# Halves of frequencies in the inverse long convolution, norms tile by tile, one merged sum on VectorE

## The reference

```
h     = rmsnorm(x) * (1 + scale1) + shift1
cq, ckv, kr, hy_in, gates = split(h @ w_in)          # 384, 256, 32, 1536, 2048 columns
q     = rmsnorm(cq) @ w_uq;  kv = rmsnorm(ckv) @ w_ukv;  kr and q's last 32 columns rotated
attn  = softmax(q k^T) v                              # 8 heads, latent: 512 queries, 640 keys
y     = v-part of short_conv(hy_in)
for o in (0, 1):                                      # bidirectional, by FFT of twice the length
    y = gate_part[o] * long_conv(y, filter[o])
merged = sigmoid(g_a) * (attn @ w_oa) + sigmoid(g_b) * (y @ w_ob)
x     = x + gate1 * (merged @ w_out)
h2    = rmsnorm(x) * (1 + scale2) + shift2
x     = x + gate2 * peer(h2)                          # 8 heads x top-16 of 128*128 single-neuron experts
```

## Time and profile before

| | us |
|---|---|
| three runs, median (lowest to highest) | 4708.16 (4695.34 to 4711.38) |
| the profiled execution, its own time | 4711.11 |
| its span | 4709.3 |
| PE busy | 3782.0 (80%) |
| DVE busy | 3191.0 (68%) |
| POOL busy | 2091.9 (44%) |
| ACT busy | 1563.4 (33%) |
| mean granted clock of TensorE, of full speed | 0.924 |

### The profile page before, as it was taken

How to read it: one execution, slowest core, us unless ns; L and a number is a source line. 1 busy time by engine, 2 the same in 40 slices (tenths; PEclk the granted TensorE clock), 3 DMA queues, 4 the chain that set the end, 5 groups by cost and what they waited for, 6 DMA issues and landing times.

```text
span 4709.3 us, 42094 instructions
## 1 busy us (share of the span) xinstructions
PE 3782.0 (80%) x12598; PEld 2025.1 (43%) x12598; DVE 3191.0 (68%) x7297; ACT 1563.4 (33%) x4531; POOL 2091.9 (44%) x1771
## 2 busy tenths in 40 slices
PE   7988799897797777767877789989698777777776
PEld 4547574446453333324533356446554232232222
DVE  1322778786898876666567768977788875755555
ACT  2321341001343444443333333100244444444444
POOL 2240355573344444454344455556144444444443
PEclk8889899998899888988989899999799899999999
DMA  7556478795899989999999877867699999999998
GB/s 276 201 205 220 174 242 304 282 354 215 327 420 406 392 364 401 417 409 380 376 421 422 317 254 262 334 240 290 233 410 412 395 416 420 418 414 421 422 421 344
DMA packets 268416, 1604.74 MB, mean 341 GB/s; under 512 B 31686, under 2 KB 34034, under 8 KB 112540
## 3 DMA queue, kind: packets, MB, share of 16 engines
q0 software_dynamic: 234880, 1395.89, 74.8%
q1 hardware_dynamic: 33308, 206.16, 11.3%
HBM read 1590.62 MB, written 11.30 MB: 340 GB/s over the span
## 4 chain that ended last, share of the span: by engine, by line
PE 34%; DMA 30%; DVE 22%; issue 5%; ACT 5%; POOL 4%; SPq 0%; DVEq 0%; ACTq 0%; POOLq 0%
DMA sb_arena<-in_peer_uv,sb_idx 14%; PE ps L1157 12%; DMA sb_gbufs<-in_peer_uv,sb_idx 11%; DVE sb_gbufs L1977 4%; PE ps L1053 4%; DVE sb_arena L1977 3%; PE ps L1094 3%; PE ps L1071 3%; DVE sb_eacc L2002 2%; POOL sb_gbufs L2223 2%; PE ps L761 2%; DMA sb_gbufs<-in_peer_uv,sb_idx_v 2%; DMA sb_ring<-in_w_oab 2%; PE ps L734 1%; ACT sb_small L1443 1%
## 5 line engine op out<-in xcount | busy, mean ns | idle before, releaser
L1157 PE MATMUL ps<-sb_gbufs,sb_dge 128*128 128x512 f32 x1836 | 909.0, 644 | 293.1 <-ACT sb_dge L1464 288.5
L1157 PE MATMUL ps<-sb_arena,sb_dge 128*128 128x512 f32 x1832 | 884.1, 631 | 248.9 <-ACT sb_dge L1464 248.8
L2237 POOL DMA_INDIRECT sb_gbufs<-in_peer_uv,sb_idx x512 | 624.9, 1221 | 890.0 <-PE ps L1157 737.4
L2237 POOL DMA_INDIRECT sb_arena<-in_peer_uv,sb_idx x512 | 615.1, 1201 | 747.5 <-PE ps L1157 648.4
L1977 DVE CUSTOM_DVE_ANT_0 sb_gbufs<-sb_gbufs,sb_keep 128x1024 f32<-128x1024 f32 x512 | 625.6, 1234 | 368.7 <-DMA sb_gbufs<-in_peer_uv,sb_idx 366.7
L1977 DVE CUSTOM_DVE_ANT_0 sb_arena<-sb_arena,sb_keep 128x1024 f32<-128x1024 f32 x512 | 622.4, 1229 | 340.6 <-DMA sb_arena<-in_peer_uv,sb_idx 338.9
L1157 PEld LDWEIGHTS ps<-sb_gbufs,sb_dge 128*128 128x128 f32 x1836 | 360.0, 205 | 804.3 <-ACT sb_dge L1464 407.1
L1157 PEld LDWEIGHTS ps<-sb_arena,sb_dge 128*128 128x128 f32 x1832 | 352.7, 200 | 746.3 <-issue 374.8
L1440 ACT ACTIVATE sb_small<-sb_small 128x2 f32<-128x2 f32 x512 | 104.1, 203 | 1503.2 <-DVE sb_small L1977 1499.6
L2223 POOL DMA_INDIRECT sb_gbufs<-in_peer_uv,sb_idx x256 | 322.2, 1259 | 324.0 <-DVE sb_small L1977 139.0
L2223 POOL DMA_INDIRECT sb_gbufs<-in_peer_uv,sb_idx_v x256 | 334.7, 1307 | 238.4 <-DVE sb_eacc L2002 181.2
(11 more groups left out here) (278 smaller groups left out, 4285.6 us busy)
## 6 DMA issues: line engine op xcount, KB each, us to landing
sb_ring<-in_w_wq SPq DMA_DIRECT2D x48, 1024.0 KB, 7.1
sb_keep<-in_w_ada POOLq DMA_DIRECT2D x52, 512.0 KB, 6.1
sb_ring<-in_w_hy SPq DMA_DIRECT2D x24, 1024.0 KB, 8.2
sb_ring<-in_w_oab SPq DMA_DIRECT2D x18, 1024.0 KB, 8.5
sb_ring<-in_w_ga SPq DMA_DIRECT2D x16, 1024.0 KB, 7.1
sb_ring<-in_w_gb SPq DMA_DIRECT2D x16, 1024.0 KB, 8.7
sb_ring<-in_w_out SPq DMA_DIRECT2D x14, 1024.0 KB, 8.2
sb_gbufs<-in_peer_uv,sb_idx POOLq DMA_INDIRECT x768, 10.2
```

The costliest lines, as they stand in the source:

```text
L1157: q = pe.matmul(ps[:, c, :], dge[:, b, :], gbuf[b][:, D + c * 512:D + c * 512 + 512], start=(h == 0 and i == 0), stop=(h == HALVES - 1 and ...
L2237: nc.gpsimd.indirect_dma_start(out=gbuf[b], out_offset=None, in_=I["peer_uv"], in_offset=bass.IndirectOffsetOnAxis(ap=idx[:, n + SLOTS:n + ...
```

## The change

Three edits.

1. In both layers' latent group, each inverse long convolution goes by halves of frequencies: for all 4 blocks of channels the matmuls of kc = 0, once that half's spectrum is there (`Yc` o*2+1); then for all 4 those of kc = 1 (`Yc` o*2+2), with the event `y_ps` after each block. The 32 matmuls, their operands and weights are the same; the four banks are all claimed ahead of the second half.
2. The query and key norms of the latent group go tile by tile: DVE waits for the two sums of squares of one tile, takes its mean and inverse root (14 small operations on 1 or 2 columns, so 56 instead of 14 in each layer), scales and rotates the tile; the `yield` stands ahead of each tile, so that the four tiles are taken at four successive points and the last at the place where all were. PE transposes a tile's three blocks once `cn` says it is done.
3. The eighth (last) merged sum of the latent group goes from POOL to DVE, right behind its two products.

```
+MERGED_BY_VECTOR = 7
...
-                pe.wait_ge(*at("cn", nt))
+                for c in range(3):
+                    claim(g.hi(c), *at("cT", c + 1))
+                for j in range(nt):
+                    pe.wait_ge(*at("cn", j + 1))
+                    for c in range(3):
+                        m = pe.transpose(ps[:, g.hi(c), j * 128:j * 128 + 128], v.cqn[:, j, c * 128:c * 128 + 128], ident[:, :])
+                        if j == nt - 1:
+                            m.then_inc(s["trc"], 1)
+                n = 3
                 if g.latent:
                     pe.wait_ge(*at("ctx", 32))
-                n = 0
-                for c in range(3):
-                    claim(g.hi(n), *at("cT", n + 1))
-                    for j in range(nt):
-                        m = pe.transpose(ps[:, g.hi(n), j * 128:j * 128 + 128], v.cqn[:, j, c * 128:c * 128 + 128], ident[:, :])
-                    m.then_inc(s["trc"], 1)
-                    n += 1
...
-                    pe.wait_ge(*at("Yc", (o + 1) * 2))
+                    def from_half(c, kc):
+                        for par in (0, 1):
+                            for r in (0, 1):
+                                m = pe.matmul(ps[:, g.lo(c), par * 256:par * 256 + 256], v.Y4[:, 2 * r + par, kc, c * 128:c * 128 + 128],
+                                              w[:, r, kc, par * 256:par * 256 + 256], start=(r == 0 and kc == 0 and par == 0), stop=(r == 1 and kc == 1),
+                                              skip_group_check=True)
+                        return m
+
+                    pe.wait_ge(*at("Yc", o * 2 + 1))
                     for c in range(4):
                         claim(g.lo(c), *at("y", o * 4 + c + 1))
-                        for par in (0, 1):
-                            for r in (0, 1):
-                                for kc in (0, 1):
-                                    m = pe.matmul(ps[:, g.lo(c), par * 256:par * 256 + 256], v.Y4[:, 2 * r + par, kc, c * 128:c * 128 + 128],
-                                                  w[:, r, kc, par * 256:par * 256 + 256], start=(r == 0 and kc == 0), stop=(r == 1 and kc == 1))
-                        m.then_inc(s["y_ps"], 1)
+                        from_half(c, 0)
+                    pe.wait_ge(*at("Yc", o * 2 + 2))
+                    for c in range(4):
+                        from_half(c, 1).then_inc(s["y_ps"], 1)
                         yield
...
-                for j in range(nt):
-                    yield
-                dve.wait_ge(*at("ss_qkv", 2 * nt))
-                mean(8, nt, QR)
-                mean(8 + nt, nt, KVR)
-                rsqrt(8, 2 * nt)
...
                 for j in range(nt):
+                    yield
+                    dve.wait_ge(*at("ss_qkv", 2 * j + 2))
+                    mean(8 + 2 * j, 1, QR)
+                    mean(9 + 2 * j, 1, KVR)
+                    rsqrt(8 + 2 * j, 2, 32 + 2 * j)
...
                     m.then_inc(s["mm"], 1)
+                    if g.latent and c >= MERGED_BY_VECTOR:
+                        dve.wait_ge(*at("mm", c + 1))
+                        dve.wait_ge(*at("mg", c))
+                        one, two = (v.mtmp[:, 2 * (c % 2) + i, 0:T] for i in (0, 1))
+                        dve.tensor_tensor(v.merged[:, c, 0:T], one, two, ALU.add).then_inc(s["mg"], 1)
...
+                    if g.latent and c >= MERGED_BY_VECTOR:
+                        yield
+                        continue
                     pool.wait_ge(*at("mm", c + 1))
```

6 lines of the change are left out of this document (3 added, 3 removed).

## The result

The changed kernel takes 4677.83 us, median of six runs (4672.71 to 4685.44), against 4703.35 of the kernel before in the same set (six runs, 4695.34 to 4711.38). The ratio is 0.9944, 95% interval 0.9933 to 0.9954: **26 us less, between 22 and 32**. Forecast was 4687 from a profiled execution of 4711.1, that is 23.7 less, with a range from 4676 to 4704; the time lies inside it, 2 us above its lower end. The gain was forecast within 2 us. The time itself is 9 us under the forecast, since the profiled execution that it starts from lies 8 us above the median of this set and not the 3 us that the prediction took.

What follows compares the result with a forecast made beforehand. PE, 80% busy, was taken as the bound, the edits being worth its waits in the latent dense stages. Terms 15.0 + 4.3 + 1.3 + 1.6 + 1.5 = 23.7 us off 4711.1 gave 4687, range 4676 to 4704.

Steps and rivals of the forecast that it cites:

- Inverse by halves: Second inverse convolution: half the matmuls move ahead of PE's last wait; 7.0 us in layer 0, 8.0 in layer 1.
- They start at 885.2: Layer 0, second inverse convolution: the first 16 matmuls start when PE fell idle, their needs done at 881.07.
- The banks are those that the first convolution used, long read: Second inverse convolution: the reason given against the first half having to wait for a bank.
- the fourth rival: Inverse's first half waits for something else, a bank or the weights; only norms and sums gain: 4702 us, chance 0.04.
- the cold end: Layer 0 inverse: second half begins at the lower clock, costs 2.5 us more, ends at 908.1; gain 7.0 us.
- the forecast's warm end: Layer 0 inverse: the shorter wait leaves the clock up, the second half ends at 905.6; gain 9.5 us.
- The `gb` wait: PE's 1.65 us wait for weights behind the layer 0 inverse: the load moves with the inverse, so the wait stays.
- Norms: Query and key norms by tile: first query rotation 4.3 us earlier in layer 1, gain 1.3 us in layer 0.
- Merged sum: Ahead of the output projection: last sum on DVE lets PE start 1.6 us earlier in layer 0, 1.5 in layer 1.
- The rival of the experts: Gathers, dots and adds on POOL and DVE set the stage and take the gain back: about 4702 us, chance 0.18.
- The clock's rival: Inverse's second half runs at the lower clock throughout, 14.0 us, in a kernel of 4698 us; chance 0.10.
- VectorE as the bound: Latent dense stage: DVE lacks slack for 8.5 us more per layer, late gathers reach the end: 4736 us, chance 0.05.

Runs made afterwards that it cites:

- halves alone: The kernel before with only the inverse long convolution by halves: 4685.5 us, ratio 0.9959.
- six sums: The changed kernel with six merged sums of the latent group on DVE instead of one: 4676.5 us, ratio 0.9946.
- without norms: The kernel before with the inverse by halves and the last merged sum on DVE, no norms tile by tile: 4686.5 us, ratio 0.9957.
- norms behind the points: The changed kernel with the four points ahead of all four norms, which stay tile by tile: 4675.5 us, ratio 0.9936.
- both orders: The changed kernel with points ahead of the norms and the second convolution's spectrum halves back to back: 4672.1 us, run again 4665.8.
- norms alone: The kernel before with only the norms tile by tile: 4696.4 us, ratio 0.9983.
- sum alone: The kernel before with only the last merged sum moved to DVE: 4695.9 us, ratio 0.9984.

## Why the prediction was right, and where not

The outcome forecast as most likely, faster by more than 0.3%, came, and the sum of 23.7 us stands against 26 measured. That they agree within 2 us is in part luck. In the one profile of the kernel before against the change's two, A to F fell by 8.6 us in layer 0, where the terms add to 9.9 (7.0 + 1.3 + 1.6), and by 16.2 in layer 1, where they add to 13.8 (8.0 + 4.3 + 1.5); and E to F alone scatters by 7 us in layer 0.

*Inverse by halves: right in kind, 15.0 forecast, 17 measured* by the marks (8.1 in layer 0 and 8.9 in layer 1, from the gates' start), 19 by the timing of halves alone. Two steps of it failed. "They start at 885.2" and "The banks are those that the first convolution used, long read" are wrong: the banks 0 to 3 belong to the forward transform's second half in between, and the claim on them held PE for 1.78 us (3.48 where the gates ended earlier). So the condition of the fourth rival, that the first half waits for a bank, came true, but not its price: the half was done before the spectrum anyway. The other step is the price of the cold end, 2.5 us for a second half that begins at the lower clock. Where that happened in layer 0 it cost 1.7 (8.86 instead of 7.14), and the gain is 7.7 instead of 7.0. In six sums and without norms the first half took the low clock instead, and the gain there is 9.4, the forecast's warm end. In layer 1 the spectrum itself came between 24.2 and 26.5 us behind the gates' start, and 26.0 to 26.1 without the halves; the change's first profile has the 24.2, and with both halves warm it gained 10.3 us there against its second's 6.5 (from the kernel before's 41.7). So the term of 8.0 can't be tested on one profile.

*Who takes the gain:* DVE's wait fell from 14.15 to 5.12 and from 15.31 to 5.75 us, 9.0 and 9.6 less, as forecast in kind and more than the 7 in size. The `gb` wait, forecast to stay, fell from 1.65 to 0.30 and from 2.20 to 1.21 us; over the other profiles it is 1.7 to 2.3 us without halves and 0.6 to 2.2 with them. Why is not shown.

*Norms: 1.3 and 4.3 forecast.* Up to the queries' projection 2.0 and 4 were measured, and the layer 1 term held. The layer 0 term did not reach the end: B to C is some 2 us longer, and the lower clock near the attention's end is the largest part of it that the traces show (2.7 us in the eight profiles that have it there). It is the same with the norms behind the points, so the late gathers are not its cause. The timings give 7 to 8 us for the edit, with an uncertainty of 6. The small operations came out as the sum had them, some 15 us more of DVE's busy time, and no cost of them is seen in the times.

*Merged sum: 3.1 forecast.* In layer 1 it gave 1.6, as forecast. In layer 0 the term of 1.6 stands on rows whose neighbourhood scatters by 7 us, and the timings say 4.4 to 7.5. What the sum gives beyond its two waits stays open; POOL's freed time is not seen as a source, since six sums did no more than one.

*The rival of the experts* was half right: PE's wait before the output projection of layer 0 is set by DVE's queue of dots and adds and their gathers, and it was 6.5 to 13.8 us, whatever the edit. That it took nothing of the gain on the whole rests on the times, 26 us against a sum of 23.7, more than on A to F of layer 0, where a scatter of 7 us hides it. *The clock's rival* was right in one thing: in most profiles one of the two halves runs its start at the lower level, which costs 1.7 us in layer 0, not the 7 us that a whole half at that level would. *VectorE as the bound* did not come. The parts alone add to 35 us and the whole is 26; with 6 us of uncertainty on each that is no contradiction, and no proof of addition either. Norms and sum without the halves were not run, so what the halves add to the other two is not measured.

## What to carry to other kernels

If a product waits for the last part of its operand, sum what is there first in PSUM; but look who holds the banks, because the claim moves forward with the matmuls. A chain of small operations ahead of a wait can be repeated per tile, here at no cost that the times showed, as long as the engine would stand there; put it where the engine stands, not between pieces that others wait for. And when a stage's wait scatters by more than the edit is worth, take the marks of several executions before pricing it, and measure from the start of a group, not from the end of one whose length the clock changes.

## What the runs showed of the hardware

TensorE's granted clock fell behind waits of 1.35 to 3.48 us, and behind the same wait it fell in one kernel or execution and not in another.

- *The two halves.* Where the wait ahead of the first was 0.41 or 0.79 us and ahead of the second 2.77, both halves took 7.14 to 7.17 us. Where the first wait was 1.73 to 2.61 and the second 2.77, the first half took 7.14 or 7.15 and the second 8.62 to 8.86, in the change at a granted clock of 0.55 at its start. Where the first wait was 3.48 (six sums, layer 0), the first half took 8.83 and the second, 1.08 us behind it, 7.17; and once (without norms, layer 1) a first wait of 2.44 did the same, 8.78 and 7.17, though halves alone had 2.44 and a first half of 7.14.
- *The gates of layer 0* stand behind a wait of 2.47 or 2.48 us and 10.54 us of forward transform in thirteen profiles. They took 15.67 us in nine (granted clock 0.54 in their first 3.6 us in the change) and 13.97 in four (1.00 in six sums). The two executions of both orders have one of each. In layer 0 the two halves follow from it: behind gates of 15.67 us the first wait is 1.78 and the second half starts low, behind gates of 13.97 it is 3.48 and the first half does.
- *The attention of layer 0* has the wait of 1.35 us told above, with a clock of 0.53 behind it in norms alone and 1.00 in sum alone, and some 2.7 us between them.

So a wait under 3 us cost 1.5 to 2.7 us or nothing. What decides it is not shown. The Trainium skill, page "TensorE: Matmul & The Clock Gate", section "HAM oscillation", tells of bursts that each start at the low clock; here at most one of the two halves did.
